# Attention on one core: scores computed once by query rows, masked on VectorE, whole-row exponentials, probabilities transposed on TensorE

## The chip, the cores and the metric

The kernel runs on one core of a Trainium2 chip. The metric is the device time of one launch in microseconds (us); lower is better. The engines are named as in the profile: PE is TensorE, PEld its weight loads, DVE VectorE, ACT ScalarE, POOL GpSimd, and SP the queue of SyncE, which here only issues DMAs.

## What is computed

One layer of a hybrid encoder for 2048 prompt tokens and 64 sample tokens (these with 1024 cached keys). It has a convolution branch and an attention branch. The change is in attention: an indexer gives each query its 256 best keys, and the softmax runs over these alone. The reference gathers the keys; the kernel works over all keys with a mask that is 0 for a selected key and -1e30 otherwise.

```python
def attend_block(q, qi, wi, qpos, k_all, v_all, ki_all, kpos, rel_bias, top_k):
    ...
    score = jnp.where(admissible[None], score, -jnp.inf)
    _, idx = lax.top_k(score, top_k)
    ...
    logits = jnp.einsum('bqhgd,bqkhd->bqhgk', qg, k_sel) * (HEAD_DIM ** -0.5)
    bias = rel_bias.astype(f32)[t5_bucket(sel_pos - qpos[None, :, None])]
    ...
    logits = jnp.where(valid[:, :, None, None, :], logits + bias, -jnp.inf)
    p = jax.nn.softmax(logits, axis=-1)
    o = jnp.einsum('bqhgk,bqkhd->bqhgd', p, v_sel)
```

There are 16 heads of 64 in 4 groups; a group of 4 query heads shares one key and value head. All matmuls that count for accuracy are done in pieces: an operand is split into a high part (fp32r) and the low rest, and the products of the parts are added in PSUM.

## The kernel before

`build` (L2562) runs five stages one after the other: front (normalised activations, keys, values), gate (all other projections, the indexer's scores, the selection of the keys into `masks`, the convolution), attention, branch and output. Each is a block in which every engine has its own instruction list; the order inside a list is fixed, and semaphores tie the lists together.

**Work of attention** (`attention_stage`, L1516). A unit is one group of heads with one tile of 128 queries (the 17th tile has the 64 sample queries): 68 units. Tiles are taken small, large, small, large (0, 15, 1, 14 and so on), then the sample's. A unit has 1 to 16 blocks of 128 keys; a block is worked for the 4 heads at once, so it is 512 columns wide (256 for the sample). Two blocks make a pair, 308 in all (580 blocks); one step of the plan handles one pair.

**Order** (`AttentionPlan`, L1423). For each step it lists what else is done: chunks of up to 512 keys of one head, which prepare a later unit (`chunks_at`, 688 in all, 2 to 4 in a busy step), and the unit's end (`copy_at`, `rows_at`, `cols_at`). The value products of a pair come two steps after its scores (LAG). All engines walk the same list of steps. Chunks, shifts, rows and columns go through a ring of 3 PSUM banks; pairs alternate between two halves of the other PSUM tensor.

**One unit before.** (1) The softmax needs the largest score of each query ahead of time. `largest` (PE, L1828 and L1846) multiplies the queries' high part with up to 512 keys, queries on the partitions; DVE (L1976, a fused add and maximum with an accumulated result) adds mask or `near` (mask plus bias of the last 256 keys, made by POOL at L1749) and keeps only the maximum. `negate` (L1979) and `shift` (L1849, with ACT's copy at L1930) turn the maxima into a row that rides in the low part of q. (2) `scores` (PE, L1768) computes the scores again with keys on the partitions: high and low products, two bias products in the last two blocks, and the mask as a product with an identity (L1784, L1787, L1794, L1796). (3) ACT takes two exponentials of the pair, one in f32 and one in fp32r (L1923, L1924); DVE subtracts them for the low part (L2021). (4) `values` (L1800) adds three products per block: high V x high p, low V x high p, high V x low p (L1815 to L1817); a column of ones in V gives the sums. (5) At the unit's end ACT copies the accumulator (L1936), PE transposes it to rows (L1864), DVE divides (L1993, L1997), PE transposes back (L1873), DVE gates (L2006), SP stores.

The steady loop of the PE is:

```python
                for k in range(2):
                    if j is not None and k < len(pairs[j][1]):
                        scores(j, k)
                    if todo:
                        largest(*todo.pop(0))
                for k in range(2):
                    if v is not None and k < len(pairs[v][1]):
                        values(v, k)
```

The whole `masks` tile (4.7 MB) stays in SBUF from the gate stage on.

## Time and profile before

| | us |
|---|---|
| median of 3 runs | 3590.76 |
| lowest and highest run | 3588.99, 3600.94 |
| span of the profiled execution | 3591.6 |
| PE busy in it | 3432.5 (96%) |
| DVE busy | 2725.5 (76%) |
| ACT busy | 1436.8 (40%) |
| POOL busy | 1142.8 (32%) |

The profiled execution has no other time than its span; it lies 0.8 us above the median of the runs. Busy shares are means over the span, so a stage is read from stretches of its own. Attention runs from about 1840 to 2957 us after the span's start. Matmuls are pipelined and their printed durations overlap: what one costs is the distance to the start of the next. The granted clock is TensorE's, 1.00 being 2.4 GHz and 0.50 being 1.2 GHz. "[x <-Y]" behind a line of the timeline is the idle time of the engine before it and what ended it.

### The profile page before, as it was taken

How to read it: one execution, taken by the hardware profiler on the slowest of the kernel's cores; microseconds unless marked ns; L12 is line 12 of the kernel's file. 1: busy time of each engine (PE TensorE's matmuls, PEld its weight loads, DVE VectorE, ACT ScalarE, POOL GpSimd, SP SyncE). 2: the span in 40 equal slices, each digit the busy share in tenths (PEclk: the TensorE clock that was granted, in tenths of full speed). 3: DMA queues.
4: the chain of work that ended last, by engine and by line, in shares of the span. 5: the costliest groups of instructions: out<-in, count | busy, mean ns of one | idle time of the engine just before them, and what ended most of it. 6: DMA issues, size and time to landing. Idle time of an engine off the chain costs nothing. (4 is left out here: it accounts for less than half of the span.)

```text
span 3591.6 us, 50100 instructions
## 1 busy us (share of the span) xinstructions
PE 3432.5 (96%) x19221; PEld 2956.8 (82%) x19311; DVE 2725.5 (76%) x4130; ACT 1436.8 (40%) x1779; POOL 1142.8 (32%) x897
## 2 busy tenths in 40 slices
PE   6989999999999899999989999999999999989998
PEld 3989888999999899999976666666666669989987
DVE  2522788999899979999968888887887765676443
ACT  2312567889800000010025555555555550234121
POOL 2222112543334000000024644634643324665200
PEclk9999999999999999999989999999999999999999
DMA  7375537455555633544443113113111106667443
GB/s 254 114 245 167 149 119 168 164 170 178 182 182 182 236 123 141 185 158 163 154 121 69 33 31 74 33 31 71 33 31 35 33 27 223 201 213 258 138 143 117
DMA packets 389540, 480.25 MB, mean 134 GB/s; under 512 B 49249, under 2 KB 315633, under 8 KB 387830
## 3 DMA queue, kind: packets, MB, share of 16 engines
q1 hardware_dynamic: 331141, 283.29, 26.9%
q10 hardware_dynamic: 48112, 157.27, 12.5%
q0 software_dynamic: 10112, 37.49, 2.6%
q8 instruction: 94, 1.54, 0.2%
q14 instruction: 81, 0.66, 0.1%
HBM read 296.97 MB, written 187.02 MB: 135 GB/s over the span
## 5 line engine op out<-in xcount | busy, mean ns | idle before, releaser
L1126 PE MATMUL psum<-ha,gt 128*128 128x352 f32 x8136 | 1352.3, 324 | 11.2 <-DVE gq_lo L1344 7.3
L1126 PEld LDWEIGHTS psum<-ha,gt 128*128 128x128 f32 x8136 | 1323.0, 189 | 14.8 <-issue 8.7
L1414 DVE SCALAR_TENSOR_TENSOR cv<-cv,vecs,cv 128x1056 f32<-128x1056 f32 (+1 forms) x480 | 598.9, 1331 | 0.0
L2021 DVE TENSOR_TENSOR at_plo<-at,at 128x1024 fp32r<-128x1024 f32 (+2 forms) x308 | 437.3, 1420 | 147.9 <-ACT at L1924 146.0
L1923 ACT ACTIVATE at<-psum 128x1024 f32<-128x1024 f32 (+2 forms) x308 | 293.1, 952 | 439.5 <-PE psum L1796 389.8
L1846 PE MATMUL psum<-at,at 128*128 128x512 f32 (+5 forms) x688 | 334.8, 496 | 20.2 <-POOL at L1731 10.0
L707 PE MATMUL psum<-br,br 128*128 128x352 f32 x2016 | 338.2, 328 | 14.5 <-DVE br L2394 10.4
L707 PEld LDWEIGHTS psum<-br,br 128*128 128x128 f32 x2016 | 331.0, 191 | 19.3 <-issue 11.7
L1749 POOL TENSOR_TENSOR at<-at,cv 128x256 f32<-128x256 f32 (+2 forms) x272 | 223.4, 824 | 366.8 <-DVE at L1976 362.8
L781 DVE TENSOR_SCALAR_CACHE_REDUCE gl<-gt,gl 128x1792 bf16<-128x1792 f32 (+8 forms) x263 | 337.7, 1350 | 1.2
L1257 ACT ACTIVATE gt<-psum 128x1056 f32<-128x1056 f32 x80 | 84.0, 1050 | 613.3 <-PE psum L1126 592.1
L752 ACT ACTIVATE gl<-gt,gl 128x2048 bf16<-128x2048 f32 (+6 forms) x224 | 314.2, 1404 | 31.2 <-DVE gl L797 27.0
L1103 POOL TENSOR_TENSOR gt<-gt,ones 128x1024 fp32r<-128x1024 f32 x60 | 123.0, 2050 | 606.3 <-PE psum L1126 593.0
L1924 ACT ACTIVATE at<-psum 128x1024 fp32r<-128x1024 f32 (+2 forms) x308 | 291.0, 945 | 0.0
L1976 DVE CUSTOM_DVE_ANT_0 at<-psum,cv 128x512 bf16<-128x512 f32 (+4 forms) x416 | 231.5, 578 | 31.0 <-PE psum L1846 27.8
L1784 PE MATMUL psum<-at,at 128*128 128x512 f32 (+1 forms) x580 | 247.1, 426 | 0.0
L1815 PE MATMUL psum<-at,at 128*65 128x512 f32 (+1 forms) x580 | 236.1, 407 | 6.2 <-ACT at L1936 3.6
L1787 PE MATMUL psum<-at,at 65*128 65x512 f32 (+1 forms) x580 | 227.0, 391 | 0.0
L1817 PE MATMUL psum<-at_plo,at 128*65 128x512 f32 (+1 forms) x580 | 224.9, 388 | 0.0
L1816 PE MATMUL psum<-at,at 128*65 128x512 f32 (+1 forms) x580 | 224.9, 388 | 0.0
L1359 DVE SCALAR_TENSOR_TENSOR gt<-gt,wi,gt 128x768 f32<-128x768 f32 (+10 forms) x168 | 187.4, 1124 | 41.5 <-ACT gt L1306 33.8
L1976 DVE CUSTOM_DVE_ANT_0 at<-psum,at 128x512 bf16<-128x512 f32 (+4 forms) x272 | 171.5, 636 | 30.5 <-PE psum L1846 24.4
(271 smaller groups left out, 4864.3 us busy)
## 6 DMA issues: line engine op xcount, KB each, us to landing
scratch_ws<-gt SPq DMA_DIRECT2D x112, 512.0 KB, 4.0
gt<-scratch_ws ACTq DMA_DIRECT2D x110, 512.0 KB, 4.9
gt<-in_w_in_dram SPq DMA_DIRECT2D x60, 512.0 KB, 5.8
scratch_gm<-gt ACTq DMA_DIRECT2D x32, 528.0 KB, 3.0
br<-scratch_gm ACTq DMA_DIRECT2D x32, 528.0 KB, 3.8
scratch_m<-br POOLq DMA_DIRECT2D x32, 528.0 KB, 5.7
at<-scratch_q SPq DMA_DIRECT2D x128, 128.0 KB, 2.9
scratch_u<-gl POOLq DMA_DIRECT2D x16, 528.0 KB, 3.7
```

The source lines that it names most:

```text
L707: last = self.nc.tensor.matmul(self.psum[b][:, j, 0:W // 3], w[b][:, c, :], a[:, c, j * (W // 3):(j + 1) * (W // 3)], start=(c == 0 and k ...
L752: nc.scalar.activation(junks[(done + k) % 2][:, 0:keys_of(t)[1]], part_of(scores, t), ACT.Sign, bias=cells["candidate"][:, j:j + 1].bitcas ...
L781: nc.vector.tensor_scalar(junks[k % 2][:, 0:keys_of(t)[1]], part_of(scores, t), threshold[:, j:j + 1].bitcast(F32), None, compare, ALU.add ...
L1126: return nc.tensor.matmul(of[:, j, 0:W // 3], part[:, c, :], a[:, c, j * (W // 3):(j + 1) * (W // 3)], start=(c == 0 and k == 0), stop=(c ...
L1414: ins = nc.vector.scalar_tensor_tensor(to[:, 0:width], mine[:, k_:k_ + width], tap, to[:, 0:width], ALU.mult, ALU.add)
L1784: nc.tensor.matmul(dst, kst[g % 2][:, keys], qhi[u % 3][:, 0:n], start=True, stop=False)
L1815: nc.tensor.matmul(acc[0:VW, 0:n], vst[g % 2][:, v, 0, :], phi[j % 3][:, k, 0:n], start=(b == 0), stop=False)
L1846: nc.tensor.matmul(bank(("max", u, h, c))[:, 0:w], qhi[u % 3][:, at:at + P], kst[g % 2][:, key0:key0 + w], start=True, stop=True).then_inc ...
L1923: nc.scalar.activation(prob[j % 3][:, 0:len(mine), 0:n], src, ACT.Exp)
L1924: nc.scalar.activation(phi[j % 3][:, 0:len(mine), 0:n], src, ACT.Exp).then_inc(s_phi, 1)
L1976: nc.vector.tensor_tensor_reduce(out=junk[r % 2][:, 0:w], in0=bank(("max", u, h, c))[:, 0:w], in1=other, scale=1.0, scalar=LOWEST, op0=ALU ...
L2021: nc.vector.tensor_tensor(plo[j % 3][:, 0:len(mine), 0:n], prob[j % 3][:, 0:len(mine), 0:n], phi[j % 3][:, 0:len(mine), 0:n].bitcast(F32), ...
```

## The change

Scores are computed once, with queries on the partitions, and kept.

- The chunk products are now high and low (`scores`), DVE adds mask or `near`, writes the negated sum as f32 to SBUF (`row_of`), and carries the running minimum from chunk to chunk (the negated maximum).
- When the last chunk of a head is done, ACT takes the exponential of the whole row in place (`exps`, up to 2048 columns), with the minimum as bias, and accumulates the sum. The exponentials stand in ACT's list one step after the last chunk, ahead of the copy of that step.
- Each block of probabilities is transposed on PE, one head at a time, into the pair's half of PSUM (`turn`). ACT copies it (high part, fp32r), DVE subtracts from PSUM (low part). `turn` of a pair waits for the subtraction of the pair two before.
- High and low part of V lie side by side in 128 columns, so that a block needs two value products (high p, low p) and not three; the two halves are added by DVE at the unit's end, in a reduction.
- The masks are no longer kept in SBUF. The gate stage stores them to DRAM on POOL's queue when the selection is done, and SP loads those of each unit into one of three buffers.
- The second key copy (`k2`), bias by columns (`bth`, `btl` and the transposed bias in DRAM), `negate`, `shift` and the ones column go. The chunks of two heads are now interleaved, the last ones may lie one step later.

The core of the diff ("..." marks what is left out):

```diff
@@ gate_stage @@
             sp.wait_ge(mem.s_bias, 16)
-            for k, name in enumerate(("bias", "biasT")):
-                to = scr[name][:, 0:P * BROW].rearrange("h (q r) -> h q r", q=P)
-                sp.dma_start(to, scr["rows"][:, k * BROW:(k + 1) * BROW].unsqueeze(1).to_broadcast([HEADS, P, BROW])).then_inc(mem.s_bias, 16)
+            sp.dma_start(scr["bias"].rearrange("h (q r) -> h q r", q=P),
+                         scr["rows"].unsqueeze(1).to_broadcast([HEADS, P, BROW])).then_inc(mem.s_bias, 16)
...
+            pool.wait_ge(s_clear, 1)
+            pool.dma_start(scr["mk"], masks[:, 0:total].bitcast(F32)).then_inc(s_mkst, 16)
             for m in range(half_pairs, 2 * half_pairs):
                 if pairs[m][1] == "u":
                     store(m)
+            pool.wait_ge(s_mkst, 16)
@@ AttentionPlan @@
-        items = [(u, h, c) for u in range(len(self.units)) for h in range(GROUP) for c in range(len(self.chunks(u)))]
+        items = [(u, h, c) for u in range(count) for a in range(0, GROUP, 2) for c in range(len(self.chunks(u))) for h in (a, a + 1)]
...
-            assert step <= self.first[u] - 3
+            assert step <= self.first[u] - 2
...
+        self.exps_at = {s: [(u, h) for w, u, h, c in placed if w == s - 1 and c == len(self.chunks(u)) - 1] for s in self.steps}
...
+        self.masks_at = at([done[u - 3] + 1 if u >= 3 else self.begin for u in range(count)])
@@ attention_stage, sync @@
+            def masks_of(u):
+                t = units[u][1]
+                at, width = score_offset(t) // 2, keys_of(t)[1]
+                if u >= 3:
+                    sp.wait_ge(s_ring, plan.final(u - 3, GROUP - 1) + 1)
+                sp.dma_start(masks[u % 3][:, 0:width].bitcast(F32), scr["mk"][:, at:at + width // 2]).then_inc(s_mk[u % 3], 16)
@@ attention_stage, tensor @@
-                nc.tensor.matmul(bank(("max", u, h, c))[:, 0:w], qhi[u % 3][:, at:at + P], kst[g % 2][:, key0:key0 + w],
-                                 start=True, stop=True).then_inc(s_rp, 1)
+                nc.tensor.matmul(bank(key)[:, 0:w], qhi[u % 3][:, at:at + P], kst[g % 2][:, key0:key0 + w], start=True, stop=False)
+                nc.tensor.matmul(bank(key)[:, 0:w], qlo[u % 3][:, at:at + P], kst[g % 2][:, key0:key0 + w],
+                                 start=False, stop=True).then_inc(s_rp, 1)
+
+            def turn(j, k):
+
+                u, mine = pairs[j]
+                n, b = plan.queries(u), mine[k]
+                if k == 0:
+                    if j == plan.first[u]:
+                        pe.wait_ge(s_exp, GROUP * (u + 1))
+                        if n == DEC:
+                            pe.wait_ge(s_pad, units[u][0] + 1)
+                    if j >= 2:
+                        pe.wait_ge(s_plo, j - 1)
                 for h in range(GROUP):
-                    last = nc.tensor.matmul(bank(("shift", u))[0:VW, h * n:(h + 1) * n], zs[u % 2][:, h, :], ident_r[:, 0:n], start=True, stop=True)
-                last.then_inc(s_zp, 1)
+                    last = nc.tensor.transpose(turned[j % 2][:, k, h * n:(h + 1) * n], row_of(u)[0:n, h, b * P:(b + 1) * P], mem.ident[0:n, 0:n])
+                if k == len(mine) - 1:
+                    last.then_inc(s_turn, 1)
+
+            def values(j, part):
...
+                of = (phi, plo)[part][j % 3]
+                for k, b in enumerate(mine):
+                    v = b if t < NT else NT + b
+                    last = nc.tensor.matmul(acc[:, 0:n], vst[g % 2][:, v, :], of[:, k, 0:n], start=(part == 0 and b == 0),
+                                            stop=(part == 1 and b == plan.blocks[u] - 1))
...
@@ attention_stage, scalar @@
+            def exps(u, h):
+
+                n, c, width = plan.queries(u), len(plan.chunks(u)) - 1, keys_of(units[u][1])[1]
+                mine = row_of(u)[0:n, h, 0:width]
+                act.wait_ge(s_ring, plan.final(u, h) + 1)
+                nc.scalar.activation(mine, mine, ACT.Exp, bias=least[0:n, u % 3, h, c:c + 1], scale=-1.0,
+                                     accum_out=total[0:n, u % plan.SUMS, h:h + 1]).then_inc(s_exp, 1)
...
             for s in plan.steps:
                 j = plan.pair(s)
+                for u, h in plan.exps_at[s]:
+                    exps(u, h)
...
-                    nc.scalar.activation(prob[j % 3][:, 0:len(mine), 0:n], src, ACT.Exp)
-                    nc.scalar.activation(phi[j % 3][:, 0:len(mine), 0:n], src, ACT.Exp).then_inc(s_phi, 1)
...
+                    nc.scalar.copy(phi[j % 3][:, 0:len(mine), 0:n], turned[j % 2][:, 0:len(mine), 0:n]).then_inc(s_phi, 1)
@@ attention_stage, vector @@
-                nc.vector.tensor_tensor_reduce(out=junk[r % 2][:, 0:w], in0=bank(("max", u, h, c))[:, 0:w], in1=other, scale=1.0, scalar=LOWEST,
-                                               op0=ALU.add, op1=ALU.max, accum_out=mx[:, u % 2, h, c:c + 1]).then_inc(s_ring, 1)
...
+                nc.vector.tensor_tensor_reduce(out=row_of(u)[0:n, h, k:k + w], in0=bank(key)[0:n, 0:w], in1=other, scale=-1.0,
+                                               scalar=least[0:n, u % 3, h, c - 1:c] if c else -LOWEST,
+                                               op0=ALU.add, op1=ALU.min, accum_out=least[0:n, u % 3, h, c:c + 1]).then_inc(s_ring, 1)
...
+                nc.vector.tensor_reduce(mine, src, axis=AX.X, op=ALU.add).then_inc(s_fold, 1)
...
-                    nc.vector.tensor_tensor(plo[j % 3][:, 0:len(mine), 0:n], prob[j % 3][:, 0:len(mine), 0:n],
+                    nc.vector.tensor_tensor(plo[j % 3][:, 0:len(mine), 0:n], turned[j % 2][:, 0:len(mine), 0:n],
                                             phi[j % 3][:, 0:len(mine), 0:n].bitcast(F32), ALU.subtract).then_inc(s_plo, 1)
```

## Rows read from the trace of the kernel before

**Rows 1.** Page: busy us, share of the span, and instructions of each engine.

```profile
span 3591.6 us, 50100 instructions
PE 3432.5 (96%) x19221; PEld 2956.8 (82%) x19311; DVE 2725.5 (76%) x4130; ACT 1436.8 (40%) x1779; POOL 1142.8 (32%) x897
```

**Rows 2.** Stretches: length, busy us and instructions per engine, clock, DMA; attention.

```profile
core 0: us, PE busy (x) PEld busy (x) DVE busy (x) ACT busy (x) POOL busy (x), PEclk, DMA share, GB/s
1900.00:2150.00 250.00, 245.55 (x1182) 158.40 (x1201) 205.83 (x466) 146.67 (x179) 131.55 (x138) 1.00 0.19 47
```

**Rows 3.** One line's instructions (ns min/median/max, first and last start); timeline, last value product.

```profile
L1784 PE MATMUL psum<-at,at x580: 274/397/793, 1875.7 to 2951.7; 128*128 128x512 f32 x182, 128*128 128x256 f32 x12
...
2954.08 0.28 PE L1817 MATMUL psum<-at_plo,at 128*65 128x256 f32 x1
```

**Rows 4.** Timeline of PE: start, length; one step of attention, and a run of products.

```profile
1894.38 0.39 PE L1784 MATMUL psum<-at,at 128*128 128x512 f32 x1
1894.61 0.40 PE L1787 MATMUL psum<-at,at 65*128 65x512 f32 x1
...
1898.04 0.40 PE L1784 MATMUL psum<-at,at 128*128 128x512 f32 x1
...
3039.72 17.64 PE L707 MATMUL psum<-br,br 128*128 128x352 f32 x108
```

**Rows 5.** Timeline of PE in the front stage: eight transposes, then the next ones.

```profile
108.10 1.03 PE L559 MATMUL psum<-ident,fr 128*128 128x128 f32 x8
108.97 0.38 PE L583 MATMUL psum<-ident,fr 128*128 128x128 f32 x2
```

**Rows 6.** Timeline of DVE: maximum chunks of 512, 384 and 512 columns in a row.

```profile
2300.03 0.69 DVE L1976 CUSTOM_DVE_ANT_0 at<-psum,cv 128x512 bf16<-128x512 f32 x1
...
2300.64 0.56 DVE L1976 CUSTOM_DVE_ANT_0 at<-psum,cv 128x384 bf16<-128x384 f32 x1
...
2301.12 0.69 DVE L1976 CUSTOM_DVE_ANT_0 at<-psum,at 128x512 bf16<-128x512 f32 x1
```

**Rows 7.** One line's instructions: the subtraction in attention, and one from PSUM in branch.

```profile
L2021 DVE TENSOR_TENSOR at_plo<-at,at x308: 426/1226/4655, 1879.5 to 2953.3; 128x1024 fp32r<-128x1024 f32 x128, 128x512 fp32r<-128x512 f32 x24, 128x256 fp32r<-128x256 f32 x2
...
L2394 DVE TENSOR_TENSOR br<-psum,br x32: 1243/1258/1260, 2993.3 to 3388.3; 128x1056 f32<-128x1056 f32 x32
```

**Rows 8.** Groups by line in attention: busy us, mean ns, idle before; the division.

```profile
L1997 DVE TENSOR_TENSOR at<-psum,at 128x256 f32<-128x256 f32 x48 | 20.4, 425 | 1.6
```

**Rows 9.** Timeline of ACT: activations with accumulated sum, and the two exponentials of a step.

```profile
598.67 2.01 ACT L752 ACTIVATE gl<-gt,gl 128x2048 f16<-128x2048 f32 x1 [0.97 <-DVE gl L792]
...
600.68 1.67 ACT L752 ACTIVATE gl<-gt,gl 128x1664 bf16<-128x1664 f32 x1
...
607.78 0.71 ACT L752 ACTIVATE gl<-gt,gl 128x512 f16<-128x512 f32 x1
...
1880.50 1.02 ACT L1923 ACTIVATE at<-psum 128x1024 f32<-128x1024 f32 x1 [1.16 <-PE psum L1796]
1881.42 1.02 ACT L1924 ACTIVATE at<-psum 128x1024 fp32r<-128x1024 f32 x1
```

**Rows 10.** Timeline of weight loads around a pause in attention; the stretch around it.

```profile
2264.26 0.32 PEld L1855 LDWEIGHTS psum<-at,at 128*65 128x65 f32 x4 [2.58 <-issue]
...
2265.49 0.34 PEld L1784 LDWEIGHTS psum<-at,at 128*128 128x128 f32 x1
2265.92 0.33 PEld L1787 LDWEIGHTS psum<-at,at 65*128 65x128 f32 x1
...
2261.00:2269.00 8.00, 5.88 (x23) 3.49 (x21) 6.31 (x11) 2.81 (x4) 3.13 (x2) 0.79 0.13 35
```

**Rows 11.** Stretch of the front stage with transposes between products.

```profile
110.00:120.00 10.00, 10.00 (x79) 10.00 (x78) 6.38 (x21) 3.92 (x6) 2.40 (x1) 1.00 0.16 48
```

**Rows 12.** Gate stage: timeline of DVE where the selection ends; the stretch behind it.

```profile
1164.96 0.20 DVE L1377 MEMSET cv<- 128x30 f32 x4
...
1170.00:1180.00 10.00, 2.66 (x9) 2.20 (x9) 4.87 (x7) 0.00 (x0) 0.00 (x0) 0.64 1.03 411
```

More of the change, by code:

```diff
@@ L1433, in __init__ @@
         self.blocks = [-(-keys_of(t)[1] // P) for _, t in self.units]
+        count = len(self.units)
         self.first, self.pairs = [], []
@@ new lines, in attention_stage @@
+        s_v, s_k, s_front, s_brow = sem("v"), sem("k"), sem("front"), sem("brow")
+        s_q, s_mk, s_ga, s_st = [sem("q0"), sem("q1")], [sem(f"mk{i}") for i in range(3)], [sem(f"ga{i}") for i in range(3)], [sem("st0"), sem("st1")]
+        s_set, s_vst, s_ktmp, s_kst, s_fhi, s_query, s_near = (sem(n) for n in ("set", "vst", "ktmp", "kst", "fhi", "query", "near"))
+        s_rp, s_ring, s_pad, s_exp, s_turn, s_phi, s_plo, s_pv = (sem(n) for n in ("rp", "ring", "pad", "exp", "turn", "phi", "plo", "pv"))
@@ L1581, in _, with row_of @@
+        def row_of(u):
+            at, n = plan.place[u], plan.blocks[u]
+            return room[:, at * Q4:(at + n) * Q4].rearrange("p (h w) -> p h w", h=GROUP)
         @block.sync
@@ L1881, in _ @@
                     if j is not None and k < len(pairs[j][1]):
-                        scores(j, k)
+                        turn(j, k)
                     if todo:
-                        largest(*todo.pop(0))
-                for k in range(2):
-                    if v is not None and k < len(pairs[v][1]):
-                        values(v, k)
+                        scores(*todo.pop(0))
+                for part in range(2):
+                    if v is not None:
+                        values(v, part)
                     if todo:
-                        largest(*todo.pop(0))
-                for u in plan.shift_at[s]:
-                    shift(u)
+                        scores(*todo.pop(0))
+                while todo:
+                    scores(*todo.pop(0))
                 for u in plan.rows_at[s]:
```

404 lines of the change are left out of this document (148 added, 256 removed).

## The prediction

> **What bounds the kernel now.** I first read the busy shares of the page: TensorE (PE) is busy 96% of the span, VectorE (DVE) 76% [rows 1]. That is a mean over five stages, and the change touches one, so I next read the table of stretches: inside attention the PE is busy 245.6 of 250 us at full clock, DVE 205.8, ScalarE (ACT) 146.7 and GpSimd (POOL) 131.6 [rows 2]. Then the source view of the score line and the last value product give the ends of the steady part: 1875.7 to 2954.2 us, 1078 us for 308 steps, 3.5 us each [rows 3]. The reader is to see that everything that takes a matmul away counts, until another engine or a chain through several engines is longer.
>
> A matmul's printed duration contains its latency; what it costs a busy PE is the distance to the next start. For 512 columns that is 0.23 us; 108 products of 352 columns take 17.64 us, 0.163 each [rows 4]. Both fit N/2400 + 0.017 us, which gives 0.124 for 256 columns. With it I count the work of before. Of 580 blocks of 128 keys, 36 (the sample's) have 256 columns. Scores: 580 x 3 and 132 x 2 for the bias; values: 580 x 3; that makes 3512 of 512 columns (808 us) and 232 of 256 (29 us). The 688 maximum products by query rows are 448 of 512 columns and 240 narrower ones, 137 us. Rows, columns and shifts of 68 units: 54 us. Sum 1028 us against 1078 measured, so 50 us of waits and unevenness lie on top. One full step shows it: 3.66 us from one pair's first product to the next one's, 16 slots of 0.23 [rows 4].
>
> **PE after.** The 688 row products are done twice (high and low part of q): 275 us. The score products by key columns, with bias, mask and shift, go. Instead each block is transposed, 4 heads, 2320 transposes (a few smaller ones for the sample). The same form, 128x128 f32 against the identity, stands in the front stage: 8 start in 0.87 us, 0.109 each [rows 5]. 580 x 4 x 0.11 = 255 us. Values: 1160 products instead of 1740, 259 us. Rows (now 4 of 128x128) and columns: 46 us. Sum 835 us, 193 less. I keep the same 50 us on top: 885.
>
> **DVE after.** The masked chunks are the same custom instruction at the same 688 widths, now written out as f32 and not bf16. Starts lie 0.61 us apart for 512 columns and 0.48 for 384, about 1.04 ns a column and 0.08 fixed [rows 6]: 308 + 54 = 362 us in all. Output type is the unknown; the trace shows no such form, and the nearest row with f32 output from PSUM is the one of the next sentence, at 1.19 ns a column with latency. So plus nothing to plus 50 us. The subtraction for the low part now reads PSUM, not SBUF. Today it has a median of 1.23 us and a maximum of 4.66, while a subtraction of 1056 columns from PSUM stays between 1.24 and 1.26 in all 32 cases [rows 7]. I take 1.14 from start to start for 1024 columns, 315 us for all. Of the unit's end, the product and the gate stay near 0.42 us each [rows 8]; added is one reduction of 512 columns from PSUM, bounded by 0.42 and 1.23, taken at 0.6; with the reciprocal about 1.5 us x 68 = 102 us. The small negation goes. Sum about 780 us, less than the PE's 835, but not by much: in the steps with a unit's end or 4 chunks it is level with it.
>
> **ACT after.** The two exponentials of 1024 columns per step (0.92 us from start to start, [rows 9]) become one copy (0.92) and the whole-row exponentials: 272 of 128 to 2048 columns. A 2048-column activation with accumulated sum, from SBUF, starts the next one after 2.01 us, a 512-column one takes 0.71 [rows 9]: 0.85 ns a column and 0.27 fixed. 296,000 columns x 0.85 ns + 272 x 0.27 = 325 us; copies 264, accumulators 34; 623 us of about 970. As a mean that costs nothing. But the exponentials come in bursts of two heads (up to 4.0 us) in ACT's queue ahead of the next copy, and behind this copy stand DVE's subtraction, the value product and the second next step's transposes, which need the PSUM pair that the subtraction frees. Before, no such queue existed.
>
> I laid one such place on the engines with these prices: steps 93 to 97, the end of the 15-block unit of group 1, with the 14-block one prepared. Zero is the PE's start of step 93. PE: 93 (3.64 us of work, 4 chunks) to 3.64, 94 (2.78, 4 chunks) to 6.44. DVE gets the third chunk of step 94 done at 6.8 and the fourth at 7.4, so ACT's exponentials of step 95 (1.79 each) run 6.8 to 8.6 to 10.4, its copy to 11.3, DVE's subtraction to 12.5. The PE does 95 and 96 (1.8 and 0.9, no chunks) by 9.15 and must wait for that subtraction with step 97: 3.3 us lost. The same working gives 3.7 us where the 16-block unit is prepared, 2.1 for the 15-block one, 2.0 for the 13-block one, about 1 for the next and nothing below. 12 us per group of heads, 4 groups: 48 us.
>
> Such a gap has a second price. After a pause of 2.58 us in the queue of weight loads, starts of 512-column products lie 0.43 us apart instead of 0.23, the 1.2 GHz level, and the mean clock of the 8 us around it is 0.79, some 1.7 us of full-speed work given away [rows 10]. 16 gaps of 2 us or more, 2 us each: 32 us. The Trainium skill ("TensorE: Matmul & The Clock Gate", Part 4) says that transpose-mode work does not count as PE activity as other matmuls do; by that the clock would fall more often than I charge, since nearly a third of the PE's work becomes transposes. The trace has, in the front stage, stretches where about one matmul in five is a transpose, and the clock there is 1.00 [rows 11]; a third it does not show.
>
> Steady part after: 835 + 50 + 48 + 32 = 965 us, against 1078: 113 us gained.
>
> **Outside the steady part.** The gate stage gains a 4.7 MB store of the masks, on the POOL queue, issued as soon as the selection ends at 1165 us. Just then the DMA engines are full (411 GB/s in 1170 to 1180) and the PE stands for the next activations: busy 2.66 of 10 us [rows 12]. 4.7 MB at 411 GB/s are 11.5 us. Bounds 0 (if the activations go first) and 15 with a cold clock; I take 9. The 3 MB bias broadcast that goes and the halved bias product were hidden behind other work: 0. At the start of attention the first chunks now need two products, and the first transposes wait for a 2.0 us exponential; but POOL and ACT have less to prepare: +2, from -3 to +6. Per-unit mask loads (up to 0.5 MB, three buffers, asked for two units ahead, some 20 us) lie beside the work: 0; SP's queue puts queries, stores and gates behind their wait, none of which is urgent. The tail has one more reduction: +1.
>
> Sum: 3591.6 - 113 + 9 + 2 + 1 = 3491 us of span. The profiled execution has a span of 3591.6 us and the runs' median is 3590.8, so nothing is to be added for the launch: 3490.
>
> **The rivals.** (a) *Everything overlaps*: the bursts are absorbed, the clock stays up, and the PE alone sets the pace. Steady 835 + 30 = 865, which gives 3390. For it: ACT has 350 us to spare. Against: only two PSUM pairs and in-order queues.
> (b) *DVE becomes the bound*: f32 output is dearer, and the reduction costs 1.2 us. 362 + 50 + 315 + 140 = 867 us of DVE work, more than the PE's 835; with its waits for ACT in the bursts (80) and the unevenness (50) 997 and with clock losses about 1015: 3541. For it: DVE was at 82% of the stretch already [rows 2]. Against: POOL no longer slows the subtraction.
> (c) *The PE loses its clock*, the case that ends slower. Mechanism: gaps of 1 to 3 us each 10 to 15 us, with transposes between them, so that the 1.2 GHz level is granted for much of the stage. Each us of PE work done at this level costs one more. I have charged 32 us. The gain of 101 us is used up when 133 of the 835 us of work, 16%, are done at the lower level. At one quarter (209 us) the time is 3490 + 177 = 3667. By the skill's sentence on transpose mode this is what would happen, and the trace's one stretch with fewer transposes speaks neither for nor against a third.
> (d) *The change doesn't do what it says*: mask loads or the room for the rows hold units back, one wait of about 1.5 us for each of 68 units: 100 us, 3590, no change. The unit three back frees both, and two units (some 25 us) lie between; unlikely.
>
> **How the numbers follow.** Chances: forecast 0.47, (a) 0.14, (b) 0.20, (c) 0.13, (d) 0.06. The forecast is 3490, with its own range of 3440 to 3530 from the bounds above (start, store, half or double the burst losses). For 8 in 10 I go down to 3410, which leaves out half of (a), and up to 3615, which takes in (b) and (d) and leaves out most of (c). A measurement of this kernel tells 0.3% from no change (10.8 us; the three runs lie within 0.33%). Faster by more than that: forecast, (a), (b): 0.81, less a little for a doubled loss in (b), 0.80. Within 0.3%: 0.06. Slower: 0.14.
>
> **What would show it.** Right: starts of transposes 0.11 us apart; PE work per step near 2.7 us; in the waits PE held by DVE's subtraction at 12 to 16 places, each right behind two long exponentials, and the granted clock down after them; DVE busy near 800 us and no subtraction over 1.3 us. Wrong if transposes in that form cost 0.2 us (+210 us of PE work), if the masked chunk of 512 columns exceeds 0.65 us, if the clock in attention falls below 0.9, or if the stretch from 1160 to 1200 grows by more than 15 us.

## The result, and the profile after

| | before | after |
|---|---|---|
| median of 4 runs, us | 3589.88 | 3501.19 |
| lowest and highest, us | 3588.97, 3600.94 | 3497.89, 3509.04 |
| span of the profiled execution, us | 3591.6 | 3498.2 |
| steady part of attention, us | 1078 | 972.6 |
| PE, DVE, ACT, POOL busy, us | 3432.5, 2725.5, 1436.8, 1142.8 | 3272.6, 2662.8, 1455.5, 1022.8 |

The ratio of the times is 0.9752, 95% interval 0.9733 to 0.9771: 89 us less. The forecast was 3490, 11 us below the median; each run is 2 us longer than its span (3500.22 for the profiled one), so against the span the forecast is 8 us low.

The page of the changed kernel, its first lines, against [rows 1]:

```profile
span 3498.2 us, 50395 instructions
## 1 busy us (share of the span) xinstructions
PE 3272.6 (94%) x19461; PEld 3013.5 (86%) x19461; DVE 2662.8 (76%) x4059; ACT 1455.5 (42%) x1945; POOL 1022.8 (29%) x881
```

The table of stretches of the changed kernel, the same 250 us as in [rows 2] (length, then busy us and instructions of PE, PEld, DVE, ACT and POOL, then the granted clock, the DMA share and GB/s):

```profile
1900.00:2150.00 250.00, 225.49 (x1331) 185.00 (x1330) 212.16 (x495) 161.54 (x231) 103.62 (x140) 0.97 0.26 66
```

Before, the PE had 4 idle us in this stretch; now it has 25, and the clock is 0.97. Its work fell further than the time did. The source views of the transposes and of the value products give the ends of the steady part, as [rows 3] did before (ns min/median/max, first and last start):

```profile
L1798 PE MATMUL psum<-ident,at x2320: 221/272/476, 1886.9 to 2858.1; 128*128 128x128 f32 x182, 64*128 64x64 f32 x12
...
L1817 PE MATMUL psum<-at,at x1160: 277/393/776, 1894.5 to 2859.5; 128*128 128x512 f32 x182, 128*128 128x256 f32 x12
```

1886.9 to 2859.5 are 972.6 us where 1875.7 to 2954.1 were 1078.3. The steady part is 105.8 us shorter, and 12.4 us are lost elsewhere, which leaves the 93.4 us of span: the gate stage's products end at 1845.5 us and not at 1834.9 (+10.7), the way from there to the first transpose took 0.5 more, and everything behind the last value product 1.2 more.

**Where the 972.6 us go.** I counted the PE's work by starts, as the prediction did: a transpose 0.11 us, a product N/2400 + 0.017. That gives 835 us; 138 us lie on top. (The count uses the prediction's own prices and takes in the 22 chunks, some 8 us, that run before the first transpose, so its agreement with the forecast tests the counts and not the prices.) Where starts lie more than 0.7 us apart, the time beyond the slot sums to 102 us: 56 before transposes, 23 before score products, 12 before value products, 11 before rows and columns. The mean granted clock of the steady part is 0.974, which gives away 26 us, and some 10 us are left in small pieces. The same working on the kernel before splits its 50 us into 30 of such gaps, 10 of clock (mean 0.990) and 10 of small pieces. So the gaps grew by 72 us and the clock's loss by 15. The view of the PE's waits in the steady part (what waited, for whom; us in total, times, longest) names the causes:

```profile
PE psum L1798 <- DVE at L1961: 47.9, 35, 3.5
PE psum L1782 <- DVE at L1942: 17.9, 19, 2.0
PE psum L1817 <- ACT at L1895: 10.5, 8, 1.8
PE psum L1837 <- DVE at L1942: 9.5, 12, 1.9
PE psum L1798 <- ACT at L1868: 2.2, 1, 2.2
```

In all its lines together the PE waits 92.5 us. Before the change the waits of the steady part summed to 28.3 us, the longest of them these:

```profile
PE psum L1846 <- POOL at L1731: 8.4, 9, 2.2
PE psum L1855 <- DVE at L2009: 4.4, 2, 2.3
PE psum L1846 <- DVE at L1997: 4.3, 5, 1.4
PE psum L1815 <- ACT at L1936: 3.6, 8, 0.9
```

The first line of the changed kernel's view is the burst that the prediction laid out. Here it is in the timelines of PE, ACT and DVE, at the place it computed (steps 93 to 97, the 14-block unit prepared):

```profile
1946.78 0.64 PE L1798 MATMUL psum<-ident,at 128*128 128x128 f32 x4
1947.17 0.71 PE L1817 MATMUL psum<-at,at 128*128 128x512 f32 x2
1951.42 0.63 PE L1798 MATMUL psum<-ident,at 128*128 128x128 f32 x4 [3.54 <-DVE at L1961]
...
1945.46 1.80 ACT L1868 ACTIVATE at<-at,at 128x1792 f32<-128x1792 f32 x1 [2.48 <-DVE at L1927]
1947.25 1.77 ACT L1868 ACTIVATE at<-at,at 128x1792 f32<-128x1792 f32 x1
1949.03 1.47 ACT L1889 CAST at<-psum 128x1024 fp32r<-128x1024 f32 x2
...
1950.04 1.82 DVE L1961 TENSOR_TENSOR at<-psum,at 128x1024 fp32r<-128x1024 f32 x2 [3.34 <-ACT at L1889]
```

Read from below: the subtraction waits for the copy, the copy stands behind two exponentials of 1.8 us, and the PE's next transposes wait for the subtraction. The PE had transposes and products up to 1947.6 and stood until 1951.4, 3.7 us by starts. The table of stretches shows the clock around it, which answers to [rows 10], and around the same place in a later group, where it was lower still:

```profile
1950.00:1958.00 8.00, 6.58 (x32) 5.58 (x33) 5.95 (x11) 3.75 (x9) 4.70 (x5) 0.79 0.36 105
...
2446.00:2454.00 8.00, 5.03 (x16) 4.28 (x17) 3.22 (x6) 4.74 (x9) 2.67 (x3) 0.59 0.39 114
```

The costs of DVE's parts stand in its groups of the steady part (busy us, mean ns, idle before):

```profile
L1961 DVE TENSOR_TENSOR at<-psum,at 128x1024 fp32r<-128x1024 f32 x256 | 311.8, 1220 | 87.1 <-ACT at L1889 86.2
L1927 DVE CUSTOM_DVE_ANT_0 at<-psum,at,at 128x512 f32<-128x512 f32 x280 | 203.9, 747 | 15.0 <-PE psum L1783 11.6 <-DVE at L1927 0.6
L1927 DVE CUSTOM_DVE_ANT_0 at<-psum,at 128x512 f32<-128x512 f32 x156 | 103.6, 685 | 13.3 <-PE psum L1783 12.2 <-POOL at L1744 0.8
...
L1939 DVE TENSOR_REDUCE at<-psum 128x256 f32<-128x512 f32 x64 | 42.3, 661 | 1.7 <-PE psum L1828 1.6
L1942 DVE TENSOR_TENSOR at<-at,at 128x256 f32<-128x256 f32 x64 | 36.8, 575 | 6.7
```

The source view of the subtraction (ns min/median/max) answers to [rows 7]: the long ones are gone.

```profile
L1961 DVE TENSOR_TENSOR at<-psum,at x308: 425/1219/1226, 1892.1 to 2858.8; 128x1024 fp32r<-128x1024 f32 x128, 128x512 fp32r<-128x512 f32 x24, 128x256 fp32r<-128x256 f32 x2
```

**The gate stage.** Timelines of POOL and PE and the stretch of [rows 12] after the change:

```profile
1164.31 0.58 POOL L1114 DMA_DIRECT2D scratch_mk<-cv  x1 [9.74 <-DVE cv L1376]
...
1182.64 3.01 PE L1125 MATMUL psum<-ha,gt 128*128 128x352 f32 x9 [14.18 <-DMA ha<-scratch_hlo]
...
1170.00:1180.00 10.00, 0.00 (x0) 0.00 (x0) 0.00 (x0) 0.00 (x0) 0.00 (x0) 0.54 1.01 431
```

The store of 4.7 MB goes out at 1164.3, and the loads of the next activations share 431 GB/s with it: the PE, busy 2.7 of these 10 us before, is busy for none of them. Its wait is 14.2 us and was 2.8.

The +10.7 us at the stage's end are not this alone, since the stretch ahead of it varies by chance. From the start of the 4601st of the stage's 8640 products, just ahead of the pause, to that of the last one, the kernel before takes 666.4 us and the changed kernel 678.2. So the store costs 11.8 us, and the changed kernel had reached that point 1.1 us earlier than the kernel before. In the seven kernels below that leave the store as it is, this stretch takes 678.1 to 679.4 us.

### The profile page after: what moved, and what is told of

The parts are those of the page before. It is cut to its first block and busy times, and to the rows that moved or that the text cites. A ratio compares the mean times of both kernels' runs of the same rounds, so it can differ in the third digit from the quotient of the medians.

```text
span 3498.2 us, 50395 instructions
## 1 busy us (share of the span) xinstructions
PE 3272.6 (94%) x19461; PEld 3013.5 (86%) x19461; DVE 2662.8 (76%) x4059; ACT 1455.5 (42%) x1945; POOL 1022.8 (29%) x881
## 3 DMA queue, kind: packets, MB, share of 16 engines
q10 hardware_dynamic: 48112, 157.22, 12.7%
## 5 line engine op out<-in xcount | busy, mean ns | idle before, releaser
L1125 PE MATMUL psum<-ha,gt 128*128 128x352 f32 x8136 | 1354.2, 325 | 22.8 <-DMA ha<-scratch_hlo 14.2
L1125 PEld LDWEIGHTS psum<-ha,gt 128*128 128x128 f32 x8136 | 1324.3, 189 | 26.8 <-DMA ha<-scratch_hlo 14.5
L1961 DVE TENSOR_TENSOR at<-psum,at 128x1024 fp32r<-128x1024 f32 (+2 forms) x308 | 346.1, 1127 | 105.5 <-ACT at L1889 104.3
L1798 PE MATMUL psum<-ident,at 128*128 128x128 f32 (+1 forms) x2320 | 348.2, 277 | 50.2 <-DVE at L1961 47.9
L1889 ACT CAST at<-psum 128x1024 fp32r<-128x1024 f32 (+2 forms) x308 | 285.4, 932 | 219.3 <-PE psum L1798 218.0
L1798 PEld LDWEIGHTS psum<-ident,at 128*128 128x128 f32 (+1 forms) x2320 | 278.1, 144 | 111.5 <-issue 52.1
L1868 ACT ACTIVATE at<-at,at 128x2048 f32<-128x2048 f32 (+16 forms) x272 | 326.1, 1201 | 113.2 <-DVE at L1927 111.9
L1817 PE MATMUL psum<-at,at 128*128 128x512 f32 (+1 forms) x1160 | 344.2, 400 | 10.7 <-ACT at L1895 10.5
L703 PEld LDWEIGHTS psum<-br,br 128*128 128x128 f32 x2016 | 331.8, 191 | 18.2 <-issue 10.7
L1782 PE MATMUL psum<-at,at 128*128 128x512 f32 (+5 forms) x688 | 295.7, 431 | 26.9 <-DVE at L1942 17.9
L1744 POOL TENSOR_TENSOR at<-at,at 128x256 f32<-128x256 f32 (+2 forms) x272 | 177.6, 656 | 434.8 <-DVE at L1927 434.2
L1927 DVE CUSTOM_DVE_ANT_0 at<-psum,at,at 128x512 f32<-128x512 f32 (+5 forms) x416 | 269.0, 674 | 15.8 <-PE psum L1783 12.3
L1817 PEld LDWEIGHTS psum<-at,at 128*128 128x128 f32 x1160 | 210.5, 193 | 48.0 <-issue 12.8
L1783 PE MATMUL psum<-at,at 128*128 128x512 f32 (+5 forms) x688 | 251.8, 367 | 0.0
L1305 ACT ACTIVATE gt<-psum 128x640 f32<-128x640 f32 (+10 forms) x192 | 153.7, 802 | 106.1 <-PE psum L1180 88.2
```

What stands on the lines that cost most here:

```text
L703: last = self.nc.tensor.matmul(self.psum[b][:, j, 0:W // 3], w[b][:, c, :], a[:, c, j * (W // 3):(j + 1) * (W // 3)], start=(c == 0 and k ...
L1125: return nc.tensor.matmul(of[:, j, 0:W // 3], part[:, c, :], a[:, c, j * (W // 3):(j + 1) * (W // 3)], start=(c == 0 and k == 0), stop=(c ...
L1782: nc.tensor.matmul(bank(key)[:, 0:w], qhi[u % 3][:, at:at + P], kst[g % 2][:, key0:key0 + w], start=True, stop=False)
L1798: last = nc.tensor.transpose(turned[j % 2][:, k, h * n:(h + 1) * n], row_of(u)[0:n, h, b * P:(b + 1) * P], mem.ident[0:n, 0:n])
L1817: last = nc.tensor.matmul(acc[:, 0:n], vst[g % 2][:, v, :], of[:, k, 0:n], start=(part == 0 and b == 0), stop=(part == 1 and b == plan.blo ...
L1868: nc.scalar.activation(mine, mine, ACT.Exp, bias=least[0:n, u % 3, h, c:c + 1], scale=-1.0, accum_out=total[0:n, u % plan.SUMS, h:h + 1]). ...
```

## The experiments

All are edits of the changed kernel. Front and gate stage differ by up to 21 us between executions of the same instructions (in the seven kernels below that leave these stages as they are, the first transpose starts anywhere from 1874.8 to 1895.7 us). So a claim on attention is read from the steady part, first transposes to last value product, against 972.6 us. It repeats well: the two kernels below that change only the store have 971.7 and 971.8 us, and the same order of exponentials gave 941.1 and 940.9 in two kernels. A median stands against the kernel before that ran beside it.

### Is the PE the bound, and does it lose its clock?

Two runs only add PE work: every score product of the high part twice, and every transpose twice.

```diff
-                for h in range(GROUP):
+                for h in (0, 1, 2, 3, 0, 1, 2, 3):
                     last = nc.tensor.transpose(turned[...
```

> The changed kernel with every transpose of a block of probabilities issued twice (same source, same place), 2320 more. Theory (PE bound, 0.11 us each): 255 us more of PE work; some of it goes into the waits that are there (about 60 us before transposes, less in the low-clock stretches), so attention grows by 190 to 240 us and the time is 3690 to 3740, with the clock in attention still above 0.95. Rival 1 (DVE or the chain through ACT sets the pace): under 100 us more. Rival 2 (transposes don't hold the clock up): with 47% of the PE's work in transposes the mean clock in attention falls below 0.85 and the growth exceeds 300 us, 3800 or more.

Measured: 3647.18 us, ratio 1.0160 (1.0124 to 1.0197); steady part 1116.7 us. That is 144 more for 255 us of work, between what the theory (190 to 240) and the first rival (under 100) gave. The stretch 1900 to 2150 of this kernel:

```profile
1900.00:2150.00 250.00, 245.06 (x1694) 217.98 (x1693) 191.88 (x424) 143.48 (x195) 89.47 (x118) 1.00 0.22 56
```

The PE is busy for 245 of 250 us, 47% of its work in the steady part (510 of 1090 us) are transposes, and the granted clock is 1.00. Over the whole steady part it is 0.99. So it is not the transposes that lowered the clock in the changed kernel; its low places lie at the pauses. What the changed kernel wastes (138 us) is down to 27: the PE's waits fall from 92.5 to 28.5 us, since the others finish while it does the extra work, and the clock's loss from 26 to 7.

```diff
-                nc.tensor.matmul(bank(key)..., qhi[...], kst[...], start=True, stop=False)
+                nc.tensor.matmul(bank(key)..., qhi[...], kst[...], start=True, stop=True)
+                nc.tensor.matmul(bank(key)..., qhi[...], kst[...], start=True, stop=False)
```

> The changed kernel with the first score product of every chunk issued twice (the first as a group of its own, overwritten), 688 more, 138 us of PE work at 0.017 us + columns/2400. Theory (PE bound in most steps): 100 to 138 us more, 3600 to 3640, the rest going into waits that are there; that also prices the third value product that the change saved (133 us). Rival (another engine sets the pace): 50 us or less.

Measured: 3578.91 us (10 runs), ratio 0.9972 (0.9954 to 0.9990); steady part 1055.2 us, 83 more for 138 us of work, waste 82. Again less than expected. Both runs say the same: a us of added PE work costs 0.56 to 0.60 us. I had expected 0.72 or more. The rest goes into pauses in which the PE waited for DVE and ACT, and into the clock that comes back with them. This is the price of one more us, not the share of the stage in which the PE is the bound.

### Which chain: the order in ACT's list

Two edits change the order alone. The first puts the pair's copy ahead of the exponentials, the second puts the exponentials last, behind the copy of the accumulators too.

```diff
                 j = plan.pair(s)
-                for u, h in plan.exps_at[s]:
-                    exps(u, h)
                 if j is not None:
 ...
                     nc.scalar.copy(phi[j % 3]..., turned[j % 2]...).then_inc(s_phi, 1)
+                for u, h in plan.exps_at[s]:      # e2_copy_first: here
+                    exps(u, h)
                 for u in plan.copy_at[s]:
 ...
                     nc.scalar.copy(accs[u % 2]..., acc...).then_inc(s_acc, 1)
+                for u, h in plan.exps_at[s]:      # e8_exps_last: here, and not above
+                    exps(u, h)
```

> The changed kernel with ACT's list in another order: in each step the copy of the transposed pair comes first and the whole-row exponentials after it. If the 57 us of waits before transposes come from the copy that stands behind two exponentials, and from nothing else, 40 to 57 us go, plus part of the low clock: 3430 to 3460. By my own layout of steps 93 to 97 the next unit's first transposes then wait for the exponentials instead (they end at 11.9 where the old order let the PE start at 12.5), so only 5 to 20 us go: 3481 to 3496, and the waits before transposes name ACT's exponential and not DVE's subtraction. I hold the second for likelier.

Measured: 3483.91 us, ratio 0.9713 (0.9673 to 0.9754); steady part 959.8 us, 12.8 less, within the 5 to 20 that were held for likelier. The PE's waits in it:

```profile
PE psum L1798 <- ACT at L1868: 30.3, 17, 2.8
PE psum L1817 <- ACT at L1895: 26.8, 23, 2.9
PE psum L1798 <- DVE at L1961: 8.9, 19, 0.8
```

The wait for the subtraction falls from 47.9 to 8.9 us, so the burst was its cause. But only a third of it is gained. A unit's first transposes now wait for the late exponentials (2.2 to 30.3), and the accumulators' copy stands behind them too: the next unit's value products wait 26.8 us for it (10.5 before). The waits for the division (L1942) fell at the same time, from 27.4 to 12.7 us. The accumulators' line gave the next edit.

> The changed kernel with ACT's list ordered copy of the pair, copy of the accumulator, and only then the whole-row exponentials. With the exponentials between the two copies the steady part shrank by 13 us, but 27 us of PE waits for the accumulator's copy came up where there had been 10. Theory: these shrink back to under 10 and 10 to 17 us more go, steady part near 945, time 3466 to 3476. Rival: the value products then wait for the exponentials' unit in another place (transposes of a unit's first pair, already 28 us), and it stays at 960.

Measured: 3470.58 us, ratio 0.9661 (0.9627 to 0.9695); steady part 941.1 us, 31.5 less, at a clock of 0.993.

```profile
PE psum L1798 <- ACT at L1868: 34.1, 21, 2.8
PE psum L1782 <- DVE at L1942: 16.1, 18, 2.4
PE psum L1798 <- DVE at L1961: 9.2, 19, 0.8
```

The value products' wait for the accumulators is gone from the list. What stays of the burst is 34 us at the start of units, where the exponentials are truly needed. All waits together fell from 92.5 to 75.5 us, and the clock's loss from 26 to 7, so more than half of the gain is clock. The longest waits are gone with it: 2.8 us at most and not 3.5.

### Giving DVE more time, in two places

The waits for DVE's division (L1942) were not in the prediction. Two plan edits try to get rid of them: columns and the store behind them one step later (`cols_at`, `gates_at`, `store_at` and `end` plus one), and 3 chunks in every step in place of 2, 2, 3 in the spread of the chunks. The diff is that of the second.

```diff
-  seen >= (3 if step % 3 == 0 else 2)
+  seen >= 3
```

> The changed kernel with the second transposition of a unit's end (cols), its gate, store and gate load each one step later. The PE of the changed kernel stands 27 us for DVE's division at a unit's end (17.9 ahead of score products, 9.5 ahead of cols), a wait that my prediction didn't name. Theory (the chain reduction, division, transposition is now too long for one step): these 27 us and a part of the low clock behind them go, attention's steady part shrinks from 973 by 20 to 35 us, time 3466 to 3481. Rival (the wait only covers another one, DVE being late anyway after the exponentials): the idle time moves to the transposes of the pairs, under 10 us gained.

> The changed kernel with chunks placed at 3 a step instead of 2 (3 in each third step), so that large units are prepared earlier and fewer steps with 4 chunks stand right before a unit's first pair. Theory (the late end of preparation makes the burst fatal): the last chunks of the four largest units still lie 3 steps ahead, since the room for them opens late, so the gaps of 3.8 and 3.5 us there stay; those of the smaller ones go: 10 to 25 us less, 3476 to 3491. Rival (a fuller mix makes DVE the bound in the steps with 3 chunks, 2.9 us against the PE's 2.9): no gain or up to 20 us more.

Columns later: 3487.50 us, ratio 0.9715 (0.9686 to 0.9744), but a steady part of 970.8 us, 1.8 less and not the 20 to 35 expected; the profiled execution is 16 us shorter mostly since its attention started 12.1 us earlier, and 11 of these were there ahead of the gate stage's store, in code that the edit leaves alone. The wait only changed its name: in the steady part PE's columns no longer wait for the division (9.5 us in the changed kernel), and its score products wait more.

```profile
PE psum L1782 <- DVE at L1942: 26.4, 27, 2.1
```

The pace: 3525.65 us, ratio 0.9808 (0.9779 to 0.9838); steady part 1000.1 us, 27.5 more. The wait for the subtraction grows from 47.9 to 67.2 us, that of score products for the division from 17.9 to 26.0. My expectation had the sign wrong. The rival written beside it had it right, but gave at most 20 us. Its reason, DVE as the bound in steps with 3 chunks, was not tested by itself.

### What DVE's chunks cost, and the bank that is freed late

```diff
-  scalar=least[0:n, u % 3, h, c - 1:c] if c else -LOWEST,
+  scalar=-LOWEST,
```

> The running minimum isn't carried from chunk to chunk: VectorE's masked chunks get a constant as start value in place of a value read from SBUF, so the minimum is that of the last chunk alone. All waits stay. In the changed kernel, 512-column chunks that carry the value lie 0.67 us apart (747 ns printed), first chunks, with a constant, 0.61 (685 ns). If the operand is the cause, all print near 685 ns, VectorE has 420 x 0.06 = 25 us less work in attention, and the median falls by 5 to 12 us, since TensorE waits for VectorE in only a part of the steps. If the wait for the chunk before is the cause (or the later chunks' other operand), they stay at 747 ns and the median at 3501.

Measured: 3483.78 us, ratio 0.9704 (0.9679 to 0.9729); steady part 958.2 us, 14.4 less. All 512-column chunks are now one group:

```profile
L1927 DVE CUSTOM_DVE_ANT_0 at<-psum,at 128x512 f32<-128x512 f32 x427 | 284.4, 687 | 34.2 <-PE psum L1783 30.4 <-DVE at L1927 0.3
```

So the 60 ns more of a later chunk is the start value read from SBUF, not the wait for the chunk before (which stayed) and not the f32 output. About 25 us of DVE work (416 x 0.06) gave 14 us of time, 0.6 of itself like the PE's. Of the 14 us some 8 are clock (0.974 to 0.982) and 3 are waits of the PE that the view names.

The other edit works on the place that e3_cols_later missed. At a unit's end DVE frees the bank of the rows after its reduction, the last that reads PSUM, and no longer after the division. It was run on top of the two edits that had gained (exponentials last, store in pieces, next part), beside these two alone.

```diff
-  nc.vector.tensor_reduce(mine, src, axis=AX.X, op=ALU.add).then_inc(s_fold, 1)
+  nc.vector.tensor_reduce(mine, src, axis=AX.X, op=ALU.add).then_inc(s_ring, 1)
 ...
-  nc.vector.tensor_tensor(mine, mine, rinv..., ALU.mult).then_inc(s_ring, 1)
+  nc.vector.tensor_tensor(mine, mine, rinv..., ALU.mult).then_inc(s_fold, 1)
```

> The kernel with exponentials last and the store in pieces, and at a unit's end VectorE frees the ring bank of the rows after its reduction (the last that reads PSUM) and no longer after the division behind it; the columns wait for the division through a semaphore of their own. Theory: TensorE's waits at the division (26 us with the exponentials last: 16 before score products, 10 before columns) hold the one part, score products that wait for the ring, which now comes 0.58 us earlier for each of some 15 to 19 places: 16 falls to about 6, steady part 941 to 931 or 935. Rival: the ring is not held by this bank but by VectorE being behind with everything, then the wait only carries another name (the reduction or a masked chunk) and the steady part stays within 3 us of 941.

Measured: 3449.86 us, ratio 0.9607 (0.9590 to 0.9623); steady part 938.2 us against 940.9 of the kernel beside it. The score products' wait for the instruction that frees the bank, without the edit (L1945 is the division there) and with it (L1942 is the reduction):

```profile
PE psum L1785 <- DVE at L1945: 16.2, 18, 2.4
```

```profile
PE psum L1785 <- DVE at L1942: 4.3, 11, 0.8
```

The wait falls by 12 us, as the theory had it, but the steady part by 2.7, which is the rival's figure. In the trace the waits that are left sum to less, while the PE's busy time is 870.6 us and not 863.8. The ring's bank was held late, yet most of that gain doesn't arrive: the PE takes longer for the same work. Its mean clock in the steady part is 0.987 against 0.993 in the kernel beside it, which is 5 us, and it may be the place of the remaining pauses and may be chance. The medians differ by 9 us, the profiled spans by 2, and the intervals overlap: the size of this gain is open.

### The store of the masks

```diff
             pool.wait_ge(s_clear, 1)
+            pool.wait_ge(pr.s_mm, QI - E + BLOCKS + 2)
             pool.dma_start(scr["mk"], masks[:, 0:total].bitcast(F32)).then_inc(s_mkst, 16)
```

> The changed kernel, with the store of the masks held back until the first two blocks of the gate stage's second half are multiplied (all activations have landed by then). Theory: the store takes its DMA time from the activations the PE stands for, some 10 us; so the PE's pause near 1170 us shrinks from 14.2 to about 3 us, the products of the gate stage end near 1835 and not 1845.5, attention is as long as in the changed kernel, and the whole is 3490 us, 10 to 11 less than the changed kernel's 3501. Rival: the longer pause is an accident of that execution or comes from the masks' loads; then nothing moves by more than 2 us.

Measured: 3497.79 us, ratio 0.9756 (0.9723 to 0.9789). No gain. The PE's waits between 1160 and 1235 us:

```profile
PE psum L1126 <- DMA gt<-scratch_ws: 9.3, 1, 9.3
PE psum L1126 <- ACT gt L1257: 5.3, 1, 5.3
PE psum L1126 <- DMA ha<-scratch_hlo: 4.1, 1, 4.1
```

The pause before the activations is down from 14.2 to 4.1 us. But the store, later, hits the load of the next weights, which has a deadline too: 9.3 us there. The stretch from the 4601st product on takes 678.6 us, as in the changed kernel (678.2). So the cost is not that of the place but of one long transfer beside a load that someone waits for. Hence eight pieces, each behind one block of products:

```diff
-            pool.dma_start(scr["mk"], masks[:, 0:total].bitcast(F32)).then_inc(s_mkst, 16)
+            cut = total // 8
+            for k in range(8):
+                pool.wait_ge(pr.s_mm, QI - E + BLOCKS + 2 + k)
+                pool.dma_start(scr["mk"][:, k * cut // 2:(k + 1) * cut // 2], masks[:, k * cut:(k + 1) * cut].bitcast(F32)).then_inc(s_mkst, 16)
```

> The changed kernel with the store of the masks in eight pieces of 0.6 MB, one behind each of the first blocks of the gate stage's second half. Held back as a whole, the store took its price elsewhere: the pause before the activations shrank from 14.2 to 4.1 us, but the PE stood 9.3 us for the next weights, which share the DMA engines. Theory (a transfer of 4.7 MB costs 10 us wherever a load with a deadline runs beside it, pieces don't): both waits are small and the gate stage's waits fall by 9 to 11 us, time 3490. Rival (the DMA work itself costs, in whatever pieces): eight waits of about 1 us, and no gain.

Measured: 3489.67 us, ratio 0.9723 (0.9696 to 0.9751), with a steady part of 971.8. Waits in the same stretch:

```profile
PE psum L1128 <- ACT gt L1259: 7.4, 1, 7.4
PE psum L1128 <- DMA ha<-scratch_hlo: 3.0, 1, 3.0
```

In both kernels one wait for ACT's activation (5.3 and 7.4 us; 6.3 in the changed kernel) stands there as well, and the kernel before has it with 6.4 us. Without it 14.2 us have become 3.0; before the change it was 2.8. The stretch from the 4601st product on takes 668.5 us (668.3 and 669.0 in the two later kernels with the pieces), 10 less than with the store in one and 2 more than before the change. The median is 11.5 us below that of the changed kernel, though the intervals of the two ratios overlap; this stretch and the waits carry the verdict.

> The two edits that shortened a stretch, together: the exponentials last in ScalarE's list of the step (steady part 972.6 to 941.1 us alone), and the masks stored in eight pieces, each behind one block of the projections (in the gate stage the wait of TensorE at the next activations fell from 14.2 to under 8 us in all). They lie in different stages. If both causes are what the single runs say, the gains add: steady part 941, gate stage 5 to 10 us shorter than in the changed kernel, median near 3462 us (3455 to 3470). If the store's cost only moves to a later stage: 3470, as with the exponentials alone.

Measured: 3459.21 us, ratio 0.9631 (0.9613 to 0.9648), steady part 940.9. The two gains add, 11.4 us below the exponentials alone (3470.58), within what was expected. With the bank freed early, 3449.86 us is the fastest version of the study: 51 us below the median of the changed kernel (which did not run beside it) and 141 below the kernel of before beside it (3591.16).

## Why the prediction held, point by point

- **PE work.** 835 us predicted, 835 counted at the same prices. The price that was new is confirmed: transposes in a row start 0.109 us apart (median of 1671), as in [rows 5]. The printed 272 ns of a transpose are mostly latency. The Trainium skill ("TensorE: Matmul & The Clock Gate", Part 4) gives about 275 ns for a bf16 one in a kernel: the printed duration of these f32 ones agrees, and a sum made with it would have been 380 us too high for 2320 of them. The price of the whole is bounded by the kernel with twice the transposes: 1090 us counted, 1117 measured.
- **The bursts.** 48 us predicted, 56 measured before transposes. Per group, from the 16-block unit prepared down: 3.7, 2.1, 3.3, 2.0 and 1 were laid out; 3.3, 3.2, 3.7, 1.9 and 1.2 stand in the trace of the second group (0.7 + 2.6, 0.7 + 2.4, then single gaps). The 15-block one was sized too low; the rest is right to 0.4 us. e2_copy_first shows that the order in ACT's queue is the cause.
- **The unevenness.** I carried over 50 us without a cause. They were 30 us of gaps, 10 of clock and 10 of small pieces. After the change the gaps that are not before transposes are 46 us, 16 more, and they aren't the old ones: waits for DVE's division (17.9 + 9.5 us, 5.8 before) and of the value products for the accumulators' copy (10.5 us, 3.6 before) make up most of them. The prediction named neither. Laying a unit's end on the engines, as it did the burst, would have found them.
- **The clock.** 32 us were charged on top of what was there. The mean over the steady part is 0.974 (0.990 before), a loss of 26 us where it had been 10: 15 more, half of the charge. The 8 us around a pause show 0.79, as in [rows 10], and the one at 2446, with the same pause, 0.59. Rival (c) fell: with nearly half of the PE's work in transposes (e4_turn_twice) the clock is 1.00 in the 250 us from 1900. The sentence of the Trainium skill ("TensorE: Matmul & The Clock Gate", Part 4) that transpose-mode work does not count as PE activity isn't borne out for these f32 transposes; the measurement decides. (The profile lists them as MATMUL and doesn't show in which mode they run.) The front-stage stretch of [rows 11] that the prediction set beside it has 11 transposes among 79 matmuls, one in seven and not one in five.
- **Luck in the sum.** The gains and losses of the steady part were forecast as 193 - 48 - 32. Measured, the gaps grew by 72 and not 48 us, and the clock's loss by 15 and not 32. Two errors of 24 and 17 us with opposite signs left one of 7.
- **DVE.** 780 us predicted from slots. Two terms were too small. Chunks that carry the minimum cost 0.06 us more (416 of them: 25 us), which the row in the trace of before could not show, as its operand was a constant. The unit's end costs 1.8 and not 1.5 us: reduction 661 ns (0.6 taken), division 575 (0.425 taken, from a form that read PSUM; [rows 8]), gate 413, 0.17 for the reciprocal. 68 x 0.3 is 20 us. Sum 825; the table of stretches has 824 busy in the steady part. f32 output cost nothing: 685 ns here, 0.69 us in [rows 6]. The subtraction is right: 1.22 us, 1.14 from start to start (the next instruction after the one at 1954.80 starts at 1955.94), 1226 ns at most.
- **Rival (b), DVE as the bound**, was half right. Its steady part of 1015 us is 42 too long, yet added PE work costs only 0.6 of itself, and DVE work taken away gives back nearly as much. By that no engine is the bound alone. The forecast's sum of PE work plus losses came out right since its losses were of the right size in all, 130 against 138, in part by the luck above.
- **Rival (a), all overlaps**: 865 us of steady part against 973, and 938 even in the best version. (d) didn't appear: no wait for mask loads is among the PE's, and the loads of `scratch_mk` need 3.2 us in the median.
- **Gate stage**: +9 predicted. The mechanism named (a store of 11 us at full bandwidth beside the activations' load) is borne out: it costs 11.8 us here and 11.7 to 13.0 in seven more kernels. The +10.7 at the stage's end also hold -1.1 us of chance ahead of it, and this could have been 10 us either way (the changed kernels reach that point from 13.2 us earlier to 7.0 later than the kernel before does). Start +2 against +0.5, behind the last value product +1 against +1.2.

An error of 7 us in the steady part and 2 in the gate stage, less 1.5 at the start, makes the 8 us between 3490 and the 3498.2 of span; the median of the runs lies 3 us above that, 2 of which every run has above its span.

## What to carry to other kernels

Lay the bursts on the engines with durations from the trace, step by step, before summing; here that gave the size of the largest loss to within 8 us. Do it at every place where work of different kinds meets in one in-order queue, the end of a unit too, and put work that is needed later behind the short copies that others wait for. Look at the clock beside the waits: the new order of ACT's list took away 17 us of waits and gave 19 more back in clock. Freeing a PSUM bank by the instruction that reads it last took 12 us of waits away here, though only 3 us of time were clear. A large store goes out in pieces if a load with a deadline may run beside it.

## What the hardware did that was not expected

- A start value read from SBUF costs the masked reduction of DVE some 60 ns at each width: 747 against 685 ns for 512 columns, 610 against 551 for 384, 478 against 417 for 256; with a constant in its place all of 512 columns take 687.
- A store of 4.7 MB cost the PE about 12 us at both places where it was tried beside a load that the PE waits for (678.1 to 679.4 us for a stretch of 666.4), and 2 to 3 us in eight pieces, each behind a block of work (668.3 to 669.0).
- The granted clock was 1.00 in a stretch of 250 us in which the PE was busy for 245, in the kernel where 47% of the PE's work in attention are transposes.
- DVE's subtraction with one operand in PSUM takes 1219 ns in the median and 1226 at most; from SBUF it had been 1226 in the median and up to 4655 [rows 7]. That GpSimd's use of SBUF beside it was the cause is only argued; no run here separates the two.
